# Four feature norms by scale, reciprocal and square root in place of logarithm and exponential

## What is computed

```
def rmsnorm(v, w):
    v32 = v.astype(jnp.float32)
    inv = lax.rsqrt(jnp.mean(v32 * v32, axis=-1, keepdims=True) + EPS)
    return (v32 * inv * w.astype(jnp.float32)).astype(v.dtype)

def _layer_norm(x, g, b):
    mu = jnp.mean(x, -1, keepdims=True)
    var = jnp.mean(jnp.square(x - mu), -1, keepdims=True)
    return (x - mu) * lax.rsqrt(var + LN_EPS) * g + b

# end of the first block
    return rmsnorm(x, final_norm_w)
# the second block, for l in 0, 1
        h = _layer_norm(DN_ALPHA * h + mix, ln1_g[l], ln1_b[l])
        f = _swiglu(...) if l % 2 == 0 else _moe(...)
        h = _layer_norm(DN_ALPHA * h + f, ln2_g[l], ln2_b[l])
```

## Time and profile before

| | |
|---|---|
| median of 3 runs | 2796.27 us (2794.53 to 2797.72) |
| the profiled execution's own time | 2792.14 us |
| its span | 2790.4 us |
| its mean granted TensorE clock | 0.969 of full |
| TensorE's matmuls busy | 2586.7 us, 93% |
| VectorE, ScalarE, GpSimd busy | 867.2, 520.4 and 369.9 us |
| table loads of ScalarE | 50 of the compiler's and 16 preloads, 1283 ns each |
| HBM traffic | 705.07 MB read, 257 GB/s over the span |

### The profile page before, as it was taken

One profiled execution on the slowest core, in us unless ns is written; L12 is line 12 of the kernel. 1 busy time (PEld: TensorE's weight loads), 2 busy tenths in 40 slices (PEclk: granted clock), 3 DMA queues, 4 the chain that ended last, 5 costly groups with the idle time before them and its releaser, 6 DMA issues.

```text
span 2790.4 us, 38613 instructions
## 1 busy us (share of the span) xinstructions
PE 2586.7 (93%) x15511; PEld 1541.5 (55%) x15511; DVE 867.2 (31%) x1612; ACT 520.4 (19%) x1063; POOL 369.9 (13%) x486
## 2 busy tenths in 40 slices
PE   7999999998999999899899779999999999899996
PEld 4446866787333433334333247787887787754442
DVE  4666155312211111111111025462001446422214
ACT  2111122300221211112112122322001323310001
POOL 2010234200110101101011100111110011100100
PEclk9999899999999999999999889999999999899998
DMA  7334320246999999999999972127443211579997
GB/s 258 127 139 152 131 91 31 91 151 278 365 419 420 419 419 420 419 420 419 420 420 419 420 281 91 35 87 262 143 151 131 91 61 61 211 298 423 423 423 305
DMA packets 165304, 720.37 MB, mean 258 GB/s; under 512 B 13076, under 2 KB 42352, under 8 KB 103552
## 3 DMA queue, kind: packets, MB, share of 16 engines
q1 hardware_dynamic: 158576, 699.44, 63.0%
q0 software_dynamic: 6144, 18.24, 1.7%
q10 hardware_dynamic: 400, 0.15, 0.0%
HBM read 705.07 MB, written 12.71 MB: 257 GB/s over the span
## 4 chain that ended last, share of the span: by engine, by line
PE 71%; SPq 14%; DMA 7%; DVE 4%; issue 2%; ACT 1%; POOL 0%; PEldq 0%; DVEq 0%; ACTq 0%; POOLq 0%
PE P L780 69%; SPq L746 13%; DMA R<-in_w_gate_up 3%; DVE R L1828 2%; PE P L783 2%; DMA R<-in_moe_w_down 1%; DMA R<-in_w_down 1%; DMA WS<-in_w_gate_up 1%; ACT R L2710 1%; DVE R L1834 1%; DMA R<-in_moe_w_up 1%; SPq L711 1%; SPq L730 1%; DMA WS<-in_w_mod 1%; POOL R L3175 0%
## 5 line engine op out<-in xcount | busy, mean ns | idle before, releaser
L780 PE MATMUL P<-R 128*64 128x512 f32 (+12 forms) x7556 | 1034.2, 435 | 88.0 <-DMA R<-in_w_down 25.6
L780 PEld LDWEIGHTS P<-R 128*64 128x64 f32 (+5 forms) x7556 | 512.5, 145 | 572.5 <-issue 415.5
L2710 ACT ACTIVATE R<-P 128x512 f32<-128x512 f32 (+3 forms) x412 | 199.8, 490 | 1745.8 <-PE P L780 1402.7
L780 PE MATMUL P<-R,WS 128*128 128x256 f32 (+1 forms) x1888 | 506.2, 427 | 7.2 <-ACT R L2710 3.0
L780 PE MATMUL P<-WS,R 128*32 128x256 f32 (+5 forms) x2840 | 461.7, 493 | 32.3 <-DMA WS<-in_w_gate_up 13.4
L780 PEld LDWEIGHTS P<-R,WS 128*128 128x128 f32 x1888 | 357.0, 191 | 140.4 <-issue 95.0
L780 PE MATMUL P<-xT,WS 128*128 128x256 f32 (+2 forms) x1728 | 400.1, 385 | 9.4 <-ACT xT L2710 3.5
L780 PEld LDWEIGHTS P<-xT,WS 128*128 128x128 f32 (+2 forms) x1728 | 317.4, 188 | 70.9 <-issue 21.0
L780 PEld LDWEIGHTS P<-WS,R 128*64 128x64 f32 (+2 forms) x2840 | 177.1, 134 | 272.8 <-issue 208.0
L1828 DVE TENSOR_TENSOR R<-P,R 128x512 f32<-128x512 f32 (+2 forms) x158 | 88.3, 573 | 541.8 <-PE P L780 457.9
L3260 POOL PARTITION_BROADCAST R<-R x180 | 120.9, 672 | 705.6 <-DMA R<-in_b_gate_up 345.6
(11 more groups left out here) (207 smaller groups left out, 877.8 us busy)
## 6 DMA issues: line engine op xcount, KB each, us to landing
R<-in_w_gate_up SPq DMA_DIRECT2D x167, 1024.0 KB, 26.5
WS<-in_w_gate_up SPq DMA_DIRECT2D x89, 1024.0 KB, 26.6
R<-in_w_down SPq DMA_DIRECT2D x85, 1024.0 KB, 26.5
WS<-in_w_in SPq DMA_DIRECT2D x60, 1024.0 KB, 7.4
WS<-in_w_down SPq DMA_DIRECT2D x43, 1024.0 KB, 26.6
R<-in_moe_w_gate SPq DMA_DIRECT2D x22, 1408.0 KB, 14.7
R<-in_moe_w_up SPq DMA_DIRECT2D x18, 1408.0 KB, 17.0
WS<-in_w_mod SPq DMA_DIRECT2D x24, 1024.0 KB, 8.1
```

The costliest lines, as they stand in the source:

```text
L780: return nc.tensor.matmul(out, lhsT, rhs, start=start, stop=stop, skip_group_check=True)
L2710: return nc.scalar.activation(out, in_, f, **kw)
```

## The change

The four norms over features take their inverse root as the norms over rows do. VectorE scales the sum of squares by 1/D and adds epsilon, out of PSUM into iv, takes the reciprocal of iv in place and counts inverse; ScalarE waits for that count and takes the square root in place. The scale also frees the PSUM bank, as the logarithm did. The tables loaded ahead of the norms are those of the square root. The last norm over rows is the eighth count of inverse in place of the fourth.

```
+            def inverse_of(stage, e):
+                n, b = ready(stage)
+                F(n, ts(iv, b[:, 0:N], 1.0 / D, e))
+                mark(v.reciprocal(iv, iv), "inverse")
+
             router(0, NEXP, TOPK)
...
+            inverse_of("ss3", 1e-6)
             rooted()
...
+                inverse_of(sa.replace("A", "B"), 1e-5)
                 rooted()
...
             def layer_norm(sb_, n, bias):
                 square(sqb, xc, n, "slice_ready", lambda k: KT * (n - 1) + k + 1)
-                log_of(sb_, 0, iv, N, 1.0 / D, 1)
-                inverse_root(iv)
+                root(iv, 3 + n)
                 shift(xT, xT, n - 1, lambda k: col(bias[0], bias[1] + k), "x_ready")
...
             sweeps(act_, a_sweep)
-            table(ACT.Ln)
+            table(ACT.Sqrt)
             square(sqb, xT, 1, "slice_ready", lambda k: k + 1)
-            log_of("ss3", 0, iv, N, 1.0 / D, 0)
-            inverse_root(iv)
+            root(iv, 4)
...
-                table(ACT.Ln)
+                table(ACT.Sqrt)
                 layer_norm(f"laB{l}", 2 + 2 * l, ("ln1_b_2", 8 * l))
...
-                    table(ACT.Ln)
+                    table(ACT.Sqrt)
                     layer_norm("lbB0", 3, ("ln2_b_2", 0))
...
-            root(st[:, 4:6], 4)
+            root(st[:, 4:6], 8)
```

## The result

The changed kernel takes 2799.98 us (median of 20 runs, 2795.66 to 2803.5), the kernel before beside it 2795.22 (20 runs, 2789.03 to 2800.71). The ratio is 1.0015 with a 95% interval of 1.0009 to 1.0021: 4.2 us more, between 2.5 and 5.9. The forecast was 2798.4 us in a range of 2793.5 to 2803, and 2.1 us more than before. The change in time is 0.15%, less than the 0.2% that the prediction took for the least that can be told; twenty runs of each kernel tell it from nothing. The profiled execution has a span of 2796.0 us against 2790.4.

The account below looks back on a forecast made before the run. The prediction took TensorE to bound the kernel (71% of the chain). Four norms at 2.78 in place of 2.26 us add 2.1 to 2792.14, giving 2794.2; with 4.1 from profiled run to median, 2798.4 us, range 2793.5 to 2803.

Parts of the forecast that it names:

- The path and its pass-through: All four norms lie on the path to the end, 4 x 2.26 = 9.0 us, each counted in full.
- The sum for a norm: Last matmul of the squared sum to VectorE's first scaling: 1.06 us plus the reciprocal, 2.78 in place of 2.26 us.
- R: Time of VectorE's reciprocal of 128x256 in each norm, taken as 1.72 us; neutral at 1.20 us.
- Rival 1: The reciprocal costs 8.2 ns an element, 2.25 us in each norm; time 2800.5 us, chance 0.17.
- Rival 2: The reciprocal streams like other operations, 0.42 us in each norm; time 2793.2 us, chance 0.07.
- The cover of 2.4 us: Behind the first norm, slack before TensorE's step reads the sigmoids, hiding a possible 1.28 us table load for layer 0's tanh.
- Rival 5: Root's table not held through the norm, or tanh's load exposed; one load per norm 5.1 us more, 2803.5, chance 0.05.
- Rival 4: TensorE's clock stays up through the router behind the last norm, 2.9 us back; time 2795.5 us, chance 0.08.
- The table rule: Skill page: one table load serves logarithm and exponential; then 7.3 us more in all; given no part or chance.
- the clock: Longer standing may lower TensorE's clock behind laB0; counted as zero, 1.3 us either way kept for the range.
- the prediction's own sign: Mechanism wrong if a table load still stood in a norm, or distances between norms changed more than the norms themselves.
- rival 3: Longer standing lowers the clock behind laB0 (2.8 us) and in lbB0 (1.5 more); 6.4 in all, 2802.7 us, chance 0.06.

Follow-up runs that it names:

- only_laB0: The kernel before with the new inverse root in stage laB0 alone, the three other norms as before; ratio to before 0.9997 (0.9987 to 1.0006).
- all_but_laB0: The kernel before with the new inverse root in ss3, lbB0 and laB1, the old one in laB0; ratio to before 1.0006 (0.9996 to 1.0015).
- three_recip: The changed kernel with three reciprocals in a row in each norm in place of one; ratio to before 1.0068 (1.0051 to 1.0085).
- one_function: The kernel before with each of the four norms' inverse root as one ScalarE activation, Abs_reciprocal_sqrt, out of PSUM; ratios to before 0.9955 and, timed again, 0.9966.

## Why the prediction was right

**The path and its pass-through.** All four norms on the path, each in full: right for a norm that gets longer, by the norms' waits and by the experts' part that doesn't change. The reading of the DMA share of 0.00 in the earlier trace rows was what mattered; the share of 1.01 behind it alone would have pointed to the other side. For a norm that gets shorter it isn't right throughout, as the 0.95 us lost in the dense stage show.

**The sum for a norm.** 1.06 + R was put together from pieces of 0.03 to 0.42 us. Measured is 2.80 - 1.753 = 1.05. That it fits to 0.01 is in part luck: VectorE starts 0.02 us behind the last matmul, not 0.10, and from the root back to VectorE are 0.11 us, not 0.03; the two misses cancel.

**R.** 1.72 forecast, 1.753 measured. The two small forms carried it, with some luck: 12 ns for 2 elements are 6.0 each and not the 6.1 of the working, which gives 1.69, and one ns more or less in that difference moves R by 0.13 us. Rival 1 (2.25) is out. What the Trainium skill, "VectorE: DVE Perf Modes", section "Walkthrough: the 8-slice pipeline in each mode", says of a repeat count of 8 can't be read as eight of the 1.03 ns steps for each element: the runs show 6.25 ns. Rival 2 (0.42) is out too.

**Table loads.** Four gone, two come, 48: right. The tanh has a load of its own, and the sigmoids behind it have another (ScalarE's timeline of the changed kernel: start us, us, instruction):

```profile
1672.03 1.28 ACT L2717 ACT_TABLE_LOAD   x1
1673.32 0.42 ACT L2717 ACTIVATE R<-R 64x256 f32<-64x256 f32 x1
1673.75 1.28 ACT L2717 ACT_TABLE_LOAD   x1
1675.05 0.86 ACT L2717 ACTIVATE R<-R 128x256 f32<-128x256 f32 x2
```

TensorE's step that reads them starts at 1678.36, 1.93 us later than in the earlier trace rows, and 1.93 us is what the path had gained in delay before. The cover of 2.4 us held. The router's load is hidden as forecast: ScalarE still stands 7.80 us behind it in place of 9.07. Rival 5 is out. Rival 4, a clock that stays up for more of the router, didn't come in the changed kernel (36.0 to 36.1 us); of all traces it is only_laB0 that shows it most, at 3.3 us. The table rule weighed in the prediction fell with the trace of before already.

**The time itself.** The forecast of 2798.4 lies 1.6 us under the measured 2799.98, closer than the change that it was made of: 2.1 us were forecast and 4.2 measured. The base helped, which is luck: the three runs of before that I started from had a median of 2796.27, all twenty of before 2795.22.

**What was missing.** The sum of 2.1 us lies just below the first measured interval of 2.5 to 5.9 and inside the second, 0 to 5.0. Two terms were not in it. The first was set to zero: the clock. "Since the same wait gave both outcomes, I count zero" is the step that the traces speak against. By the prediction's own sign, stretches between the norms that change by more than the norms do, this part of the mechanism was not right. A wait of 3.5 us left the clock up behind laB0 in three of six traces, one of 3.9 to 4.0 us in none of five, and where it falls the matmuls behind take 1.7 to 2.8 us more in the changed kernel, not the 1.3 that I took from lbB0. Averaged over the traces that is 2.0 us for this stretch, and 1.0 more by the one behind ss3, of which the stretch behind lbB0 gives 1.5 back; with four and three traces none of these means is firm. Half of rival 3 came: the fall behind laB0, at the price it named for that place, but behind lbB0 nothing longer in the changed kernel than in before, which would have carried the whole to its 2802.7.

The second term is small and steady. All three traces of the changed kernel have 0.40 us in place of 0.05 before VectorE's mean in laA0, and a wait in laB1 that is 0.28 us longer than the same pieces in lbB0. Both are time for which the profile shows no releaser. The first is also in all_but_laB0, but not in three_recip; the second is in three_recip and one_function, but not in all_but_laB0. They come and go with the kernel's code and not from run to run. A fetch of instructions by DMA would suit that, but the trace of the changed kernel has no packet of its instruction queues between 1901 and 1902 nor between 2422 and 2425. Their cause stays open.

With this second term 2.1 + 0.35 + 0.28 is 2.7 us without any clock, which both timings allow (2.5 to 5.9 and 0 to 5.0). How much the clock adds over many executions stays open: the traces give the price of a fall, but seven of them don't give how often it comes.

## What to carry to other kernels

Price an operation that the trace has only in tiny forms by the difference of two of its own forms: 12 ns between 2 and 4 elements gave 1.72 us for 256, and 1.753 came; a larger form, where there is one, makes that slope less a matter of single ns. In a stage where TensorE stands and waits, count the wait as well for what its clock does behind it: in the traces with 0.5 us more of waiting up to 2.8 us more stood behind one norm, and with 1.7 us less the clock was at its upper level behind three norms. Before two functions are traded for three cheaper ones, look for the one function that is their product: one activation made the same step in 0.53 us, where both versions took 2.3 and 2.8.

## What the runs showed of the hardware

- VectorE's reciprocal of float32 takes 152 + 6.25 n ns for n elements in each partition (4 to 512, run sizes), six times the 1.03 ns for each element of a sum of two tensors.
- The function Abs_reciprocal_sqrt takes 0.47 us for 128x256 out of PSUM (run one_function), as long as the logarithm in the earlier trace rows.
- Behind a wait of 1.2 to 1.8 us (ss3, laB0, lbB0 of one_function) the granted clock was 1.00 for the next 10 us in both traces of that kernel; behind 2.9 us (ss3) it fell in all seven traces; behind 3.5 us it fell to 1.2 GHz in three of six traces at laB0, and in all seven at lbB0; behind 3.9 to 7.9 us it fell in every trace. Behind laB1 it fell at 2.03 us too.
- Four profiled executions of one kernel differ by 4.5 us in span (before: 2790.4 to 2794.9). By the table up to 2.5 us of that lie ahead of the first norm, where I did not follow them, and up to 3.5 between lbB0 and laB1; the four waits and the experts' part are the same to 0.4 us.
